# A hybrid RG-LRU, HGRN2 and mixture-of-experts layer on one core: the vector engine's head loop written out, and four pieces of work put elsewhere

## The chip, the core and the metric

The kernel runs on one core of one Trainium2 chip. The metric is the device time of one execution in microseconds (us). The core has a matrix engine (TensorE: PE for its matrix products, PEld for its weight loads), VectorE (DVE), ScalarE (ACT), GpSimd (POOL) and SyncE (SP), which here issues nearly all transfers from the chip's memory. Every engine runs its own program in order, and the programs meet in semaphores: one engine waits until another has counted a semaphore up far enough.

## The reference

One backbone layer on 256 latent tokens and 256 context tokens, width 1024, all in float32. Cut to what matters:

```python
hx = modulate(rmsnorm(x), ...);  hc = modulate(rmsnorm(ctx), ...)      # shift and scale from c @ w_mod
ax, ayx, qx, ffx, fbx, vx, ogx, gax, gbx = split(hx @ w_in)            # the same w_in for hc
ya = RG-LRU of the convolved a, forward and backward                   # 8 heads of 128 channels
yb = HGRN2 of q, f, v, forward and backward, in chunks of 32 tokens    # 8 heads of 128 x 128
pa = (ya * gelu(ay)) @ w_proj_a;  pb = (headnorm(yb) * silu(og)) @ w_proj_b
x  = x + gate1 * ((sigmoid(ga) * pa + sigmoid(gb) * pb) @ w_out)
h2 = modulate(rmsnorm(x), ...)
x  = x + gate2 * moe(h2)      # 4 groups of 8 experts, best group, its best two experts per token
out = rmsnorm(x) * final_g
```

The context is used only for the states from which the latent scans start. `w_mod` has 6 x 1024 columns; the first 2048 are needed ahead of the heads, the other 4096 (gates, second shift and scale) are worked out beside the heads, 512 columns in each head.

## The kernel before, in words

The program has four stages. A short one normalises and turns the tokens. Then come the eight **heads**, one after another. Then the two **projections** with `w_proj_a` and `w_proj_b`, tile m of 128 output columns from 0 to 7, the merge and the product with `w_out`. Last is the **expert stage**: every expert's three weight matrices (2 MB each) pass through a ring of ten buffers.

The order of the work is written out by hand on each engine; there is no scheduler. What sets it in a head:

- **PE** makes the products with `w_in` for the head. Line 732 (`down_k`) is a whole product over eight blocks of 128 rows. Line 804 (`product`) is half of one: the forget gates of latent and context tokens are made in seven half products (FG1 to FG7) instead of eight, with sums of weight blocks and sums of token blocks. Lines 818 and 819 are the RG-LRU gate products of direction 0 and 1, which need the convolved `u` (DVE line 1658). Line 876 (`value_product`) does the same trick for the values `v`, two heads at a time: in an **even** head five such half products, in an **odd** head two. After the values come the transposed keys (825), the attention blocks (838 to 856), the row sums of the modulation (755), and the products with the state (864).
- **DVE** copies the head's parameters (1645), convolves (1656, 1658), adds up the forget gates out of the bank sums (1682, the outputs `fg_out` OUT15, OUT16, OUT_FC, OUT_BC, OUT_BX), forms the decays, and at the end of the head scans (1749) and writes the two results `ya_g` and `yb_g` (line 1854). Between the forget-gate sums it works on the modulation: `mod_products(first, end)` multiplies blocks `first` to `end` of the 512 `w_mod` columns by a scalar and adds them to block 0 (line 1670 for block 0, 1672 for the others). They are eight operations in a head in all, each waiting for the one ahead, and the last raises `modr_out`, for which PE's row sums at line 755 wait. `ratios(d)` is three operations: add (1730), reciprocal (1731), multiply (1732). `evacuate(d)` takes the masked attention blocks of direction d out of the bank (1785, 1788, and for d = 1 line 1791). Line 1836 picks the modulation rows out of the bank and raises `mod_out`.
- **POOL** multiplies gate and `u` for each direction (`gates(d)`, line 675), forms products with the decays (`prods`), the sums of forget-gate weights for the next head (`weight_sums`, 652 to 657), and the scan inputs (`inputs`, 691). `value_sums` (662, 664, 666, 667) forms the four sums of value weights for a pair of heads; PE's second value product needs the first two of them, its fifth all four.
- **SP** issues each transfer when its buffer is free.

DVE's heads are a loop with two heads in its body (odd and even are different code), so four passes; POOL's are a loop of three passes of two, and the last two heads are written out.

```python
with dve.Fori(0, HEADS - 1, 2) as h:
    for odd in range(2):
        head(h + odd, h, odd)
```

Of the kernel before, what the change touches and what calls it, by code (L numbers as in the profile page):

```python
# [22 lines left out]
P = 128  # L23
KT = D // P
# [62 lines left out]
def build(nc, x, c, ctx_in, c_ctx, w_mod, b_mod, norm1_g, w_in, conv_w, conv_b, lru_wa, lru_ba, lru_wx, lru_bx,  # L87
# [9 lines left out]
    with ExitStack() as es:  # L97
# [19 lines left out]
        def S(name):  # L117

            if name not in sems:
                sems[name] = es.enter_context(nc.semaphore(name))  # L120
            return sems[name]
# [225 lines left out]
        def this(h, d=None):  # L347
            return h + 2 if d is None else 2 * h + d + 3

        def last(h, d=None):  # L350
            return h + 1 if d is None else 2 * h + d + 1
# [42 lines left out]
        def _(sp):  # L394
# [134 lines left out]
            def proj_loads(m):  # L529

                if m >= 4:
                    sp.wait_ge(S(f"proj_mm{m % 2}"), m // 2 - 1)
                sp.dma_start(wp[m % 4][0], wpa_v[:, :, P * m:P * m + P]).then_inc(S(f"wp_in{m % 4}"), 16)
                sp.dma_start(wp[m % 4][1], wpb_v[:, :, P * m:P * m + P]).then_inc(S(f"wp_in{m % 4}"), 16)
# [13 lines left out]
            proj_loads(3)  # L548
            sp.wait_ge(S("yb_out"), this(HEADS - 1))
            sp.wait_ge(S("ya_out"), this(HEADS - 1))  # L550
            for i in range(2):
                sp.dma_start(wo[i], wo_v[:, :, F * i:F * i + F]).then_inc(S("wo_in"), 16)
            proj_loads(4)
            proj_loads(5)
            proj_loads(6)
            proj_loads(7)
            fetch(2)
# [52 lines left out]
        def _(pool):  # L610
# [48 lines left out]
            def value_sums(pair):  # L659

                pool.wait_ge(S("in_v"), (pair + 2) * 16)
                pool.tensor_tensor(vs1, v21, v22, ALU.add).then_inc(S("v_w"), 1)
                pool.wait_ge(S("v_w"), v_w_at(pair, 1))
                pool.tensor_tensor(vs2, vs1, v11, ALU.subtract).then_inc(S("v_w"), 1)
                pool.wait_ge(S("v_w"), v_w_at(pair, 2))
                pool.tensor_tensor(vs4, v12, vs2, ALU.subtract).then_inc(S("v_w"), 1)
                pool.tensor_tensor(vs3, v11, v21, ALU.subtract).then_inc(S("v_w"), 1)

            def head(h, more):

                def gates(d):

                    pool.wait_ge(S("ig_out"), this(h, d))
                    pool.wait_ge(S("conv_out"), this(h))
                    pool.tensor_tensor(ig[d], ig[d], u, ALU.mult).then_inc(S("iu_out"), 1)  # L675

                def prods(d):
                    pool.wait_ge(S("ec_out"), this(h, d))
                    pool.tensor_tensor(ec[d], ec[d], kk[d][:, T:], ALU.mult)
                    pool.wait_ge(S("exps_out"), this(h, d))  # L680
                    pool.wait_ge(S("qs_out"), this(h))
                    pool.tensor_tensor(e3[d], e3[d], qs, ALU.mult).then_inc(S("qe3_out"), 1)
                    pool.wait_ge(S("fac_out"), this(h, d))
                    pool.wait_ge(S("qe3_out"), this(h, d))
                    pool.tensor_tensor(chunks(q0[d]), chunks(e3[d]), per_chunk(fac[d][:, 2, :]), ALU.mult).then_inc(S("q0_out"), 1)

                def inputs(d):

                    pool.wait_ge(S("sqrt_out"), this(h, d))
                    pool.wait_ge(S("iu_out"), this(h, d))  # L690
                    pool.tensor_tensor(tz[d], tz[d], ig[d], ALU.mult).then_inc(S("b_out"), 1)

                gates(0)
                gates(1)
                prods(0)
                prods(1)
                if more:
                    pool.wait_ge(S("lv_out"), this(h, 1))
                    weight_sums(h + 1)
                inputs(0)  # L700
                inputs(1)
# [5 lines left out]
            pool.wait_ge(S("hx_out"), KT + 3)  # L707
            pool.tensor_tensor(ht4, x_hi, ht2, ALU.subtract).then_inc(S("tok_copy"), 1)
            with pool.Fori(0, HEADS - 3, 2) as h:
                value_sums(h)  # L710
                head(h, True)
                head(h + 1, True)
            value_sums(HEADS - 2)
            head(HEADS - 2, True)
            head(HEADS - 1, False)

            pool.wait_ge(S("rstd_out"), 3)
# [830 lines left out]
        def _(dve):  # L1548
# [87 lines left out]
            def head(h, pair, odd):  # L1636
# [40 lines left out]
                def fg_sum(dst, bank_, other, n_mm, n_out, needs=None):  # L1677

                    dve.wait_ge(S("fg_mm"), fg_at(h, N_FG, n_mm))
                    if needs:  # L1680
                        dve.wait_ge(S("fg_out"), fg_at(h, N_FG_OUT, needs))
                    tt(dst, bank_[:, 0:T], other, ALU.add).then_inc(S("fg_out"), 1)  # L1682
# [2 lines left out]
                dve.wait_ge(S("prod_q"), last(h, 1))  # L1685
                dve.wait_ge(S("qe3_out"), last(h, 1))
                tt(qs, PJ[1][:, 0:T], sq, ALU.mult).then_inc(S("qs_out"), 1)
                fg_sum(fg15, TB, fg1, FG5, OUT15)
                mod_products(0, 2)
                fg_sum(fg16, KB, fg1, FG6, OUT16)  # L1690
                mod_products(2, 5)
                fg_sum(gg[0][:, T:], TB, fg16, FG3, OUT_FC, OUT16)
                mod_products(5, 6)
                fg_sum(gg[1][:, T:], KB, fg15, FG7, OUT_BC, OUT15)

                def forget(d):
# [27 lines left out]
                    tt(d4[d].rearrange("p (c s) -> p c s", s=CH),  # L1724
                       lc[:, :, tot:tot + 1].to_broadcast([P, NCH, CH]), lc, ALU.subtract).then_inc(S("lc_out"), 1)

                def ratios(d):

                    dve.wait_ge(S("tz_out"), this(h, d))
                    link(ts(rc[d], tz[d], 1.0, None, ALU.add))  # L1730
                    link(dve.reciprocal(rc[d], rc[d]))
                    tt(tz[d], tz[d], rc[d], ALU.mult).then_inc(S("w_out"), 1)

                def prods(d):
# [57 lines left out]
                    i.then_inc(S("att_out"), 1)  # L1792

                forget(0)
                mod_products(6, 7)
                fg_sum(gg[1][:, 0:T], KB, fg1, FG4, OUT_BX)
                mod_products(7, KT).then_inc(S("modr_out"), 1)
                forget(1)
                def values(dst, bank_, other, n_mm, needs=None):

                    dve.wait_ge(S("v_mm"), v_at(pair, n_mm))
                    if needs:
                        dve.wait_ge(S("v_out"), v_at(pair, needs))
                    if dst is v_x or dst is v_c:
                        dve.wait_ge(S("inter_mm"), last(h, 1))
                    if other is None:
                        i = cp(dst, bank_[:, 0:T])
                    else:
                        i = tt(dst, bank_[:, 0:T], other, ALU.add)
                    i.then_inc(S("v_out"), 1)  # L1810
# [18 lines left out]
                    values(v_c, TB, v16, V3)  # L1829
                prods(1)  # L1830
                levels(1)
                ratios(0)
                evacuate(0)
                dve.wait_ge(S("mod_mm"), this(h))
                dve.wait_ge(S("mod_out"), last(h))
                stt(mod_acc, OB[:, 0:P], col(V_PICK), mod_acc, ALU.mult, ALU.add).then_inc(S("mod_out"), 1)
                evacuate(1)
                ratios(1)
                scans(0)
# [14 lines left out]
                stt(yb_g[:, h, :], on, col(V_HG), sog, ALU.mult, ALU.mult).then_inc(S("yb_out"), 1)  # L1854
                assert link.n == N_STEP, link.n

            with dve.Fori(0, HEADS - 1, 2) as h:
                for odd in range(2):
                    head(h + odd, h, odd)


            def merge(i, b, first):
# [325 lines left out]
```

## Time and profile before

| | |
|---|---|
| median of 3 runs | 975.27 us (971.31 to 975.5) |
| the profiled execution, its own time | 970.89 us |
| its span in the trace | 968.8 us |
| PE busy | 810.9 us, 84% |
| DVE busy | 416.5 us, 43% |
| ACT busy | 271.2 us, 28% |
| POOL busy | 133.8 us, 14% |
| transfers | 285.68 MB, 295 GB/s over the span |

The span is the time from the first to the last instruction of the profiled execution. "Busy" counts the engine's own work; an engine that waits for a semaphore is idle. The shares are averages over stages with different limits: the heads end at about 434.6 us, the projections and the product with `w_out` at about 522 us, and the rest is the expert stage.

### The profile page before, as it was taken

The page shows a single profiled execution, that of the slowest core. Times are in us where ns is not written, and L with a number is a line of the kernel's source. Part 1 is how long each engine was busy: PE and PEld are TensorE (multiplying, and loading weights), DVE is VectorE, ACT ScalarE, POOL GpSimd, SP SyncE. Part 2 cuts the span into 40 slices and gives each one's busy share as a digit, 9 for nine tenths or more (in the row PEclk, how much of TensorE's full clock was granted, in tenths as well). Part 3 has the DMA queues.
Part 4 walks back from the last instruction along what each step waited for, and adds up shares of the span by engine and source line. Part 5 has one row for each costly group of instructions (what it writes and reads, how often), then busy time and mean ns, then how long its engine had stood idle before and what let it go on. Part 6 is the DMA issues. An engine that isn't in the chain of part 4 may idle for free.

```text
span 968.8 us, 13449 instructions
## 1 busy us (share of the span) xinstructions
PE 810.9 (84%) x4788; PEld 538.5 (56%) x4788; DVE 416.5 (43%) x973; ACT 271.2 (28%) x547; POOL 133.8 (14%) x157
## 2 busy tenths in 40 slices
PE   3989998999899989999999856574865646799796
PEld 1678887888788879888857322122231301333432
DVE  3687797769676968782125610401001000010102
ACT  5344454445343635360005111001010100101202
POOL 1453151306040514120000000000000000000000
PEclk9999999999999999999999997688887877899999
DMA  9945472446344634479986999999999999999996
GB/s 369 320 104 184 110 218 78 150 133 206 86 126 139 199 95 124 135 237 365 360 340 249 377 428 427 429 426 429 426 429 428 427 427 428 428 428 429 426 423 255
DMA packets 128568, 285.68 MB, mean 295 GB/s; under 512 B 6944, under 2 KB 101376, under 8 KB 114816
## 3 DMA queue, kind: packets, MB, share of 16 engines
q1 hardware_dynamic: 127424, 283.56, 77.6%
q10 hardware_dynamic: 1088, 1.43, 0.4%
q8 instruction: 28, 0.46, 0.2%
q14 instruction: 28, 0.23, 0.1%
HBM read 283.91 MB, written 1.06 MB: 294 GB/s over the span
## 4 chain that ended last, share of the span: by engine, by line
PE 48%; DMA 31%; DVE 8%; issue 5%; SPq 3%; ACT 2%; POOL 2%; ACTq 1%; DVEq 0%; POOLq 0%
DMA arena<-in_w 29%; PE bank L732 12%; PE bank L1137 9%; PE bank L804 8%; PE bank L876 4%; PE bank L1046 3%; PE bank L1148 3%; PE bank L1012 2%; DMA arena<-in_w_proj_b 2%; SPq L591 1%; DVE arena L1672 1%; DVE arena L1774 1%; PE bank L764 1%; PE bank L818 1%; PE bank L819 1%
## 5 line engine op out<-in xcount | busy, mean ns | idle before, releaser
L1137 PE MATMUL bank<-arena 128*32 128x512 f32 (+1 forms) x1024 | 146.9, 679 | 80.3 <-DMA arena<-in_w 80.3
L732 PE MATMUL bank<-arena 128*128 128x256 f32 (+1 forms) x896 | 204.7, 379 | 0.1
L732 PEld LDWEIGHTS bank<-arena 128*128 128x128 f32 x896 | 167.8, 190 | 23.9 <-issue 0.4
L1137 PEld LDWEIGHTS bank<-arena 128*32 128x32 f32 (+1 forms) x1024 | 39.4, 127 | 185.5 <-issue 99.6
L2010 DVE TENSOR_TENSOR arena<-arena,bank 128x512 f32<-128x512 f32 x9 | 9.3, 1034 | 237.5 <-PE bank L1137 237.5
L804 PE MATMUL bank<-arena 128*128 128x256 f32 x448 | 102.6, 383 | 4.7 <-DVE arena L1682 4.7
L1148 PE MATMUL bank<-arena 128*32 128x512 f32 (+1 forms) x512 | 74.6, 683 | 31.8 <-DMA arena<-in_w 31.8
L804 PEld LDWEIGHTS bank<-arena 128*128 128x128 f32 x448 | 85.0, 191 | 18.3 <-DVE arena L1682 3.8
L719 POOL TENSOR_TENSOR arena<-arena,rstd 128x512 f32<-128x512 f32 x1 | 1.0, 1041 | 529.0 <-DVE rstd L2152 529.0
L2019 DVE TENSOR_TENSOR arena<-bank,arena 128x512 f32<-128x512 f32 x18 | 12.5, 692 | 127.6 <-PE bank L1148 127.6
L1148 PEld LDWEIGHTS bank<-arena 128*32 128x32 f32 (+1 forms) x512 | 19.5, 127 | 79.9 <-issue 47.0
L1498 ACT ACTIVATE arena<-bank 128x512 f32<-128x512 f32 x9 | 5.4, 597 | 191.7 <-PE bank L1137 191.7
L876 PE MATMUL bank<-arena 128*128 128x128 f32 x448 | 52.0, 275 | 0.0
L876 PEld LDWEIGHTS bank<-arena 128*128 128x128 f32 x448 | 51.6, 192 | 0.4
L1672 DVE SCALAR_TENSOR_TENSOR arena<-arena 128x512 f32<-128x512 f32 x56 | 46.8, 836 | 0.8
L1502 ACT ACTIVATE arena<-bank 128x256 f32<-128x256 f32 x9 | 3.4, 383 | 138.0 <-PE bank L1199 138.0
L1490 ACT ACTIVATE arena<-bank,arena 128x128 f32<-128x128 f32 x72 | 27.0, 456 | 30.5 <-PE bank L1124 30.5
L1124 PE MATMUL bank<-arena 128*128 128x128 f32 x288 | 33.8, 276 | 1.3 <-DVE arena L1990 1.3
L1124 PEld LDWEIGHTS bank<-arena 128*128 128x128 f32 x288 | 32.9, 192 | 3.1 <-DVE arena L1990 2.2
L675 POOL TENSOR_TENSOR arena<-arena 128x258 f32<-128x258 f32 x16 | 16.0, 1004 | 128.5 <-ACT arena L1354 128.5
L1158 PE MATMUL bank<-arena 128*128 128x512 f32 x64 | 29.6, 605 | 0.0
L1012 PE MATMUL bank<-arena 128*128 128x256 f32 x128 | 29.0, 380 | 0.4 <-DMA arena<-in_w_proj_b 0.4
(343 smaller groups left out, 1079.7 us busy)
## 6 DMA issues: line engine op xcount, KB each, us to landing
arena<-in_w SPq DMA_DIRECT2D x89, 2048.0 KB, 29.2
arena<-in_w_in SPq DMA_DIRECT2D x72, 512.0 KB, 5.1
arena<-in_w_mod SPq DMA_DIRECT2D x11, 2048.0 KB, 11.3
arena<-in_w SPq DMA_DIRECT2D x10, 1024.0 KB, 14.4
arena<-in_w_proj_a SPq DMA_DIRECT2D x8, 512.0 KB, 7.1
arena<-in_w_proj_b SPq DMA_DIRECT2D x8, 512.0 KB, 7.2
arena<-in_w_out SPq DMA_DIRECT2D x2, 2048.0 KB, 15.5
arena<-in_x SPq DMA_DIRECT2D x4, 512.0 KB, 9.2
```

The costliest lines, as they stand in the source:

```text
L675: pool.tensor_tensor(ig[d], ig[d], u, ALU.mult).then_inc(S("iu_out"), 1)
L732: i = mm(dst, w(k), rhs(k), start=k == 0, stop=k == KT - 1)
L804: i = mm(dst[:, 0:T], w[:, k, :], rhs[:, k, :], start=fresh and k == 0, stop=k == HALF - 1, skip_group_check=True)
L876: i = mm(dst[:, P * t:P * t + P], tokens[:, k, P * t:P * t + P], w[:, k, :], start=fresh and k == 0 and t == 0, stop=k == HALF - 1, skip_g ...
L1012: mm(PJ[1 - b][:, 0:T], wp[m % 4][0][:, k, :], ya_g[:, k, :], start=k == 0, stop=k == KT - 1)
L1046: i = mm(bank[to][:, 0:wide], merged[:, k, P * t:P * t + P], wo[c0 // F][:, k, c0 % F:c0 % F + wide], start=k == 0, stop=k == KT - 1)
L1124: i = mm((GX if half else UX)[:, P * k:P * k + P], xn[t][:, P * kt:P * kt + P], hot[:, t, :], start=t == 0, stop=t == 1)
L1137: i = mm(acc[w * b:w * b + w, :], xg[:, k, w * b:w * b + w], wtile(kind, b, u)[:, k, :], start=k == 0, stop=k == KT - 1)
L1148: i = mm(acc[w * b:w * b + w, :], gT[:, f, w * b:w * b + w], wtile("w2", b, u)[:, f, 512 * hf:512 * hf + 512], start=f == 0, stop=f == F / ...
L1158: i = mm(ACC[t][hf][:], ct[:, t, :], ys[:, hf, :], start=u == 0, stop=False, skip_group_check=True)
L1490: i = A(xg[:, kt, :], (GX if half else UX)[:, P * k:P * k + P], ACT.Identity, scale=mod_pk[:, 1, kt:kt + 1], bias=mod_pk[:, 0, kt:kt + 1])
L1672: i = stt(acc, wmod[:, k, :], c_k, acc, ALU.mult, ALU.add)
```

## The change

Four edits.

1. **DVE's head loop is written out**: the same function is called eight times with numbers in place of a loop register, so that the branch back and the register arithmetic for waits are gone. In the program DVE has 862 rows instead of 497.
2. **In the first head DVE works in another order.** OUT16 comes right behind OUT15, blocks 0 and 1 of the modulation behind it, then the other forget-gate sums with nothing between them; block 2 follows `forget(1)`, and blocks 3 to 7 stand behind `ratios(0)`, ahead of `evacuate(0)`. In the odd heads (1, 3, 5, 7) `evacuate(0)` and line 1836 stand ahead of the multiply that ends `ratios(0)`.
3. **POOL forms the value sums of a pair inside the even head**, between `gates(0)` and `gates(1)`, instead of ahead of it, which was right behind the odd head's `inputs(1)`.
4. **SP issues the two `w_out` transfers** behind the projection weights of tiles 4 and 5 instead of ahead of them.

```diff
@@ block.sync
             sp.wait_ge(S("yb_out"), this(HEADS - 1))
             sp.wait_ge(S("ya_out"), this(HEADS - 1))
+            proj_loads(4)
+            proj_loads(5)
             for i in range(2):
                 sp.dma_start(wo[i], wo_v[:, :, F * i:F * i + F]).then_inc(S("wo_in"), 16)
-            proj_loads(4)
-            proj_loads(5)
             proj_loads(6)
             proj_loads(7)
@@ block.gpsimd
-            def head(h, more):
+            def head(h, more, pair=None):
...
                 gates(0)
+                if pair is not None:
+                    value_sums(pair)
                 gates(1)
...
             with pool.Fori(0, HEADS - 3, 2) as h:
-                value_sums(h)
-                head(h, True)
+                head(h, True, h)
                 head(h + 1, True)
-            value_sums(HEADS - 2)
-            head(HEADS - 2, True)
+            head(HEADS - 2, True, HEADS - 2)
             head(HEADS - 1, False)
@@ block.vector
+                first = h == 0
                 fg_sum(fg15, TB, fg1, FG5, OUT15)
+                if first:
+                    fg_sum(fg16, KB, fg1, FG6, OUT16)
                 mod_products(0, 2)
-                fg_sum(fg16, KB, fg1, FG6, OUT16)
-                mod_products(2, 5)
+                if not first:
+                    fg_sum(fg16, KB, fg1, FG6, OUT16)
+                    mod_products(2, 5)
                 fg_sum(gg[0][:, T:], TB, fg16, FG3, OUT_FC, OUT16)
-                mod_products(5, 6)
+                if not first:
+                    mod_products(5, 6)
                 fg_sum(gg[1][:, T:], KB, fg15, FG7, OUT_BC, OUT15)
...
-                def ratios(d):
+                def ratios(d, between=None):
...
                     link(dve.reciprocal(rc[d], rc[d]))
+                    if between:
+                        between()
                     tt(tz[d], tz[d], rc[d], ALU.mult).then_inc(S("w_out"), 1)
...
                 forget(0)
-                mod_products(6, 7)
+                if not first:
+                    mod_products(6, 7)
                 fg_sum(gg[1][:, 0:T], KB, fg1, FG4, OUT_BX)
-                mod_products(7, KT).then_inc(S("modr_out"), 1)
+                if not first:
+                    mod_products(7, KT).then_inc(S("modr_out"), 1)
                 forget(1)
+                if first:
+                    mod_products(2, 3)
...
-                ratios(0)
-                evacuate(0)
-                dve.wait_ge(S("mod_mm"), this(h))
-                dve.wait_ge(S("mod_out"), last(h))
-                stt(mod_acc, OB[:, 0:P], col(V_PICK), mod_acc, ALU.mult, ALU.add).then_inc(S("mod_out"), 1)
+                def first_out():
+                    evacuate(0)
+                    dve.wait_ge(S("mod_mm"), this(h))
+                    dve.wait_ge(S("mod_out"), last(h))
+                    stt(mod_acc, OB[:, 0:P], col(V_PICK), mod_acc, ALU.mult, ALU.add).then_inc(S("mod_out"), 1)
+
+                if odd:
+                    ratios(0, first_out)
+                else:
+                    ratios(0)
+                    if first:
+                        mod_products(3, KT).then_inc(S("modr_out"), 1)
+                    first_out()
...
-            with dve.Fori(0, HEADS - 1, 2) as h:
-                for odd in range(2):
-                    head(h + odd, h, odd)
+            for h in range(HEADS):
+                head(h, h - h % 2, h % 2)
```

How the instructions stand now. First DVE in head 0, from the product `qs` (line 1687) on; 1682 is a forget-gate sum, 1670 and 1672 are modulation blocks, `ISA` and `REGISTER_ALU` serve the waits of the loop. Before:

```order
L1687 TENSOR_TENSOR arena<-bank,arena 128x256
L1679 ISA
L1682 TENSOR_TENSOR arena<-bank,arena 128x256
L1665 REGISTER_ALU
L1670 TENSOR_SCALAR arena<-arena 128x512
L1560 REGISTER_ALU
L1672 SCALAR_TENSOR_TENSOR arena<-arena 128x512
L1560 REGISTER_ALU
L1679 REGISTER_ALU
L1682 TENSOR_TENSOR arena<-bank,arena 128x256
L1672 SCALAR_TENSOR_TENSOR arena<-arena 128x512
```

After (1706 and 1707 are `forget`, lines 1701 and 1702 before):

```order
L1687 TENSOR_TENSOR arena<-bank,arena 128x256
L1682 TENSOR_TENSOR arena<-bank,arena 128x256 x2
L1670 TENSOR_SCALAR arena<-arena 128x512
L1672 SCALAR_TENSOR_TENSOR arena<-arena 128x512
L1682 TENSOR_TENSOR arena<-bank,arena 128x256 x2
L1706 TENSOR_SCALAR arena<-arena,hp 128x512
L1707 TENSOR_SCALAR arena<-arena 128x512
L1682 TENSOR_TENSOR arena<-bank,arena 128x256
L1706 TENSOR_SCALAR arena<-arena,hp 128x512
L1707 TENSOR_SCALAR arena<-arena 128x512
L1672 SCALAR_TENSOR_TENSOR arena<-arena 128x512
```

Six modulation blocks have left the place between the forget-gate sums: one stands at the end here, five further down. Second, DVE in an odd head, where `ratios(0)` and `evacuate(0)` meet; 1785, 1788 and 1836 became 1792, 1795 and 1848, and 1730 to 1732 became 1735, 1736 and 1739. Before:

```order
L1730 TENSOR_SCALAR arena<-arena 128x258
L1560 REGISTER_ALU
L1731 RECIPROCAL arena<-arena 128x258
L1560 REGISTER_ALU
L1732 TENSOR_TENSOR arena<-arena 128x258
L1785 COPY_PREDICATED arena<-head_tab,bank 128x256
L1788 COPY arena<-bank 128x2x128
L1836 SCALAR_TENSOR_TENSOR arena<-bank,hp,arena 128x128
```

After:

```order
L1735 TENSOR_SCALAR arena<-arena 128x258
L1736 RECIPROCAL arena<-arena 128x258
L1792 COPY_PREDICATED arena<-head_tab,bank 128x256
L1795 COPY arena<-bank 128x2x128
L1848 SCALAR_TENSOR_TENSOR arena<-bank,hp,arena 128x128
L1739 TENSOR_TENSOR arena<-arena 128x258
```

The multiply moved behind line 1848. Third, POOL at the start of an even head (here the last one), as a difference; 675 is `gates`, 662 to 667 are the value sums:

```order
+L675 TENSOR_TENSOR arena<-arena 128x258
 L662 TENSOR_TENSOR arena<-arena 128x512
 L664 TENSOR_TENSOR arena<-arena 128x512
 L666 TENSOR_TENSOR arena<-arena 128x512
 L667 TENSOR_TENSOR arena<-arena 128x512
-L675 TENSOR_TENSOR arena<-arena 128x258 x2
+L675 TENSOR_TENSOR arena<-arena 128x258
 L679 TENSOR_TENSOR arena<-arena 128x256
```

The four value sums stood ahead of both gate products and now stand between them.

## Rows read from the trace of the kernel before

**Rows 1.** Windows: PE, PEld, DVE, ACT, POOL busy, clock, DMA share, GB/s.

```profile
152.43:251.66 99.23, 96.34 (x564) 84.39 (x565) 77.13 (x168) 46.79 (x92) 30.38 (x32) 1.00 0.49 144
...
570.00:968.00 398.00, 280.02 (x1718) 103.96 (x1710) 38.85 (x99) 42.09 (x101) 1.04 (x1) 0.86 0.99 418
```

**Rows 2.** Waits of PE over the whole span: total, times, longest.

```profile
PE bank L1137 <- DMA arena<-in_w: 80.3, 12, 11.1
...
PE bank L818 <- DVE arena L1658: 7.5, 3, 2.6
...
PE bank L804 <- DVE arena L1682: 4.7, 2, 3.4
...
PE bank L864 <- DVE arena L1836: 1.0, 3, 0.3
...
PE bank L1012 <- DMA arena<-in_w_proj_b: 0.4, 1, 0.4
```

**Rows 3.** Waits of DVE for issue, over the whole span.

```profile
DVE hp L1645 <- issue: 9.7, 3, 4.0
...
DVE arena L1656 <- issue: 7.0, 3, 2.5
```

**Rows 4.** Timeline of DVE, end of head 3 and start of head 4.

```profile
235.10 0.74 DVE L1749 TENSOR_TENSOR_SCAN arena<-arena 128x256 f32<-128x256 f32 x1
...
236.48 1.74 DVE L1749 TENSOR_TENSOR_SCAN arena<-arena 128x256 f32<-128x256 f32 x1 [0.64 <-POOL arena L691]
...
243.00 0.49 DVE L1854 SCALAR_TENSOR_TENSOR arena<-arena,hp 128x256 f32 x1 [0.16 <-DVE arena L1851]
...
246.41 0.18 DVE L1645 COPY hp<-par 128x23 f32 x1 [2.92 <-issue]
...
249.04 0.61 DVE L1656 TENSOR_SCALAR arena<-arena,hp 128x256 f32<-128x256 f32 x2 [2.45 <-issue]
```

**Rows 5.** Timeline of POOL, head 3's gates(1) and the first value sum for head 4.

```profile
210.79 1.26 POOL L675 TENSOR_TENSOR arena<-arena 128x258 f32<-128x258 f32 x1 [5.10 <-ACT arena L1354]
...
236.40 1.27 POOL L662 TENSOR_TENSOR arena<-arena 128x512 f32<-128x512 f32 x1
```

**Rows 6.** Timeline of PE, head 4's first gate product.

```profile
251.66 0.70 PE L818 MATMUL bank<-arena 128*128 128x258 f32 x2 [2.56 <-DVE arena L1658]
```

**Rows 7.** Timeline of DVE, modulation products early in head 0.

```profile
49.12 2.54 DVE L1672 SCALAR_TENSOR_TENSOR arena<-arena 128x512 f32<-128x512 f32 x1
...
52.13 4.21 DVE L1672 SCALAR_TENSOR_TENSOR arena<-arena 128x512 f32<-128x512 f32 x3
```

**Rows 8.** Timeline of PE, its two waits in head 0.

```profile
52.31 1.97 PE L804 MATMUL bank<-arena 128*128 128x256 f32 x8 [1.35 <-DVE arena L1682]
...
58.52 3.58 PE L804 MATMUL bank<-arena 128*128 128x256 f32 x8 [3.37 <-DVE arena L1682]
```

**Rows 9.** Timeline of POOL, one value sum in head 0.

```profile
52.87 1.42 POOL L664 TENSOR_TENSOR arena<-arena 128x512 f32<-128x512 f32 x1
```

**Rows 10.** Timeline of DVE, head 0, last operation of ratios(0).

```profile
80.14 0.94 DVE L1732 TENSOR_TENSOR arena<-arena 128x258 f32<-128x258 f32 x1
```

**Rows 11.** Timeline of POOL, last weight sum in head 0.

```profile
82.17 1.27 POOL L657 TENSOR_TENSOR arena<-arena 128x512 f32<-128x512 f32 x1
```

**Rows 12.** Timeline of PE, head 0, the modulation row sums.

```profile
83.80 0.42 PE L755 MATMUL bank<-arena,ones 128*32 128x128 f32 x8
```

**Rows 13.** Timeline of DVE, head 3, a modulation product and the last forget-gate sum.

```profile
210.71 0.74 DVE L1672 SCALAR_TENSOR_TENSOR arena<-arena 128x512 f32<-128x512 f32 x1
...
211.97 0.42 DVE L1682 TENSOR_TENSOR arena<-bank,arena 128x256 f32<-128x256 f32 x1 [0.51 <-PE bank L804]
```

**Rows 14.** Timeline of PE, head 2, its five value products.

```profile
164.64 9.09 PE L876 MATMUL bank<-arena 128*128 128x128 f32 x80
```

**Rows 15.** Timeline of DVE, head 2, the first value sum out.

```profile
169.34 0.42 DVE L1809 TENSOR_TENSOR arena<-bank,arena 128x256 f32<-128x256 f32 x1
```

**Rows 16.** Timeline of SP, issue of the fifth w_proj_a tile.

```profile
445.23 2.99 SPq L533 DMA_DIRECT2D arena<-in_w_proj_a  x1
```

## The prediction

> **What bounds the kernel now.** I read the busy times by stretch first. In one pair of heads PE works 96.3 of 99.2 us at full granted clock, DVE 77; in the expert stage the DMA engines are busy 0.99 of the time and PE 280 of 398 us [rows 1]. So the heads are PE's and the experts are the memory's. The list of PE's waits says what PE still loses: 7.5 us in three waits at line 818 for the convolution, 4.7 us in two at line 804 for forget-gate sums, 1.0 us in three at line 864 for line 1836, 0.4 us at line 1012 for projection weights; the 80.3 us at line 1137 are the expert weights [rows 2]. Only those first four, 13.6 us in all, can be won by moving other engines' work. Then I read what makes DVE late at the three waits. In the whole span it has 9.7 us and 7.0 us of idle time "for issue" at lines 1645 and 1656, three times each [rows 3]: nothing was awaited, instructions did not come. The timeline shows the place: `yb_g` of head 3 is done at 243.5, the parameter copy starts at 246.41 after 2.92 us of nothing, the convolution at 249.04 after another 2.45 [rows 4]. That is the loop's branch back; inside a pass, between heads of the same pair, no such row exists. PE gets to its gate product at 251.66 - 2.56 = 249.10 and waits for the convolution [rows 6].
>
> **Edit 1, the loop written out.** It removes three branches back, with 16.7 us of DVE time [rows 3]. PE gets from them what it waits, 7.5 us [rows 2], no more. Check of what is late next: from the start of the convolution to PE's product are 251.66 - 249.04 = 2.6 us [rows 4, 6]; started at about 243.8, it is done by 246.4, 2.7 us ahead of PE. So the whole 7.5 goes, and even a fetch pause of 2.5 us left at this place would cost nothing. Term: **-7.5**; bounds -7.5 and 0.
>
> **Edit 3, the value sums.** What leaves the odd head's end: beside the first sum (236.40 to 237.67) DVE's scan took 1.74 us instead of 0.74 [rows 4, 5]. It ended at 238.22, 0.55 behind the sum's end: it stood until POOL's operation was over, and then ran. This helps only the path that edit 1 has already freed; it adds at least 1.0 us to the 2.7 of slack and nothing to the sum. What arrives: POOL's gap ahead of `gates(1)` is 5.10 us in head 3 [rows 5], and four sums take 4 x 1.27 = 5.1 alone, 4 x 1.42 = 5.7 beside DVE's modulation products [rows 5, 9]. They start where the gap starts, 210.79 - 5.10 = 205.7, and end near 211.4. DVE has two forget operations and a modulation product (0.74 at 210.71) to do ahead of the sum OUT_BX at 211.97, with 0.51 us of idle between [rows 13]. If line 1702 stands until 211.4, then takes 0.3, and the product stands behind `gates(1)` (0.6) and takes 0.55, OUT_BX starts near 212.9, 0.9 late. The chain from there (sigmoid, logarithm, scans, value sum) has little slack: PE's fourth value product of five starts at about 164.64 + 3/5 x 9.09 = 170.1, and DVE's sum for it ends at 169.76 [rows 14, 15], 0.3 us. So 0.6 us a head. This holds for heads 2, 4 and 6: **+1.8**. Bounds: 0, if DVE gets in between two sums; above, if each side stands for the whole of the other's operation, the five operations of DVE and the six of POOL in this stretch come one after another and OUT_BX is 1.9 late, 1.6 x 3 = 4.8. I take the lower middle, because beside DVE POOL's sums grew only from 1.27 to 1.42 [rows 9].
>
> The Trainium skill (SBUF — State Buffer, "Who interferes with whom") speaks against this edit: a VectorE instruction with two SBUF inputs and a GpSimd instruction that reads SBUF lock each other out for a whole instruction, whoever starts first. The scan agrees for DVE's side; POOL's 1.42 is less than the page would give. By the page alone the sum below would be -6.1 instead of -9.1.
>
> **Edit 2, the first head.** PE's two waits of 1.35 and 3.37 us are here [rows 8]. They come from modulation products beside POOL: 2.54 us for one, 4.21 for three, instead of 0.74 [rows 7, 13], in front of the sums that PE needs. Put ahead of them, OUT16 can be made as soon as PE's product for it is done, and OUT_BC needs only PE's next one; both waits go: **-4.7**. The price stands later. Five modulation products now stand behind `ratios(0)`, and PE's row sums at 83.80 wait for the last. In the time of the old trace: `ratios(0)` ends at 81.08 [rows 10]; the first product stands behind POOL's third weight sum (until 82.2), ends at 82.75; the second behind the fourth, 82.17 + 1.27 = 83.44 [rows 11], ends at 84.0; three more of 0.77 end at 86.3. PE waits 86.3 - 83.8 = 2.5 [rows 12], where before DVE was idle. Term **+2.5**; bounds 0.7 (five times 0.77 from 80.6, POOL in no one's way) and 4.3 (five times 1.40 from 81.1). The value sums beside `forget` in this head: 0.2 more. In the odd heads line 1836 goes ahead of a multiply that takes 0.94 beside POOL [rows 10], so `mod_out` comes about 1 us earlier and the waits of 0.33 end: **-1.0**. The multiply ends about 1 us later, but its reader on ACT is behind two table loads and POOL's `inputs` behind the weight sums.
>
> **Edit 4, w_out.** Tile 4's weights, issued at 445.23 [rows 16], stood behind 4 MB in the queue; ahead of them they come in time: **-0.4**. The `w_out` weights come later by about the 10 us that 4 MB take at 418 GB/s [rows 1], but still ahead of tiles 6 and 7 in the same queue, which PE needs first. So nobody can wait for them. The expert loads behind have the same bytes ahead of them as before.
>
> **Does the end move?** The expert stage is bound by its transfers, whose start is set by buffers that PE and DVE free. When those events come earlier, the whole stream does. Head time therefore passes to the end one for one.
>
> **Sum.** -7.5 - 4.7 - 1.0 - 0.4 + 1.8 + 2.5 + 0.2 = **-9.1 us**. The profiled execution's own time is 970.89, two us above its span and 4.4 below the median of the runs, 975.27; two of the three runs lie near 975. Nothing in one profile explains that difference, so I take the saving from the median: **966 us** (from the profiled execution it is 961.8). With the bounds of edits 2 and 3 the saving is 4.3 to 12.7.
>
> **Rivals.**
> - *The value sums stall the even heads* by the whole-operation lock: saving 6.1 or less, 969. For it: the scan's 1.74 us; against: 1.42 for POOL. 0.15, a fifth of it under 0.5%.
> - *The larger saving*: DVE slips between POOL's operations and the five products cost 0.7: 12 us, 963. Against it: 4.21 us for three products. 0.10.
> - *The saving stays in the heads.* If a transfer that doesn't hang on PE bounded the expert stage, the time would be 975 as before. For it: 0.99 DMA share. Against: the ring's loads wait for PE there. 0.09.
> - *Slower: instructions come late in the straight code.* 862 rows instead of 497, none of them repeated, have to be fetched beside the weights. One late fetch of 2.5 us [rows 4] in each head, in the stretch with 0.3 us of slack, costs 8 x 2.2 = 17.6: 975.3 + 8.5 = 984. It decides from 1.1 us in each head. Against it: all of DVE's large pauses for issue are at the branch [rows 3], and the first pass through the loop's body, which was new code too, has none. 0.06.
> - The forecast itself, a saving of 6.5 to 11.5: 0.60.
>
> No change can be told from 0.5% (4.9 us) here. Faster by more: 0.60 + 0.10 + 0.12 = 0.82. Within: 0.03 + 0.09 = 0.12. Slower: 0.06. The range goes from 958.5, the largest saving from the lower level of the runs, to 971.5, the smallest from the median.
>
> **What would show it.** DVE's list of waits without "issue" at 1645 and 1656; PE without the wait at 818, with none at 804 in head 0 and a new one of about 2.5 us at 755 in head 0; value sums of 1.3 to 1.7 us inside even heads, and PE waits of 0.6 us at line 876 in heads 2, 4 and 6; pairs of heads of about 96.9 us instead of 99.2. The prediction is wrong if new pauses for issue stand in the middle of heads, if PE waits over 1.5 us at 876, or if the expert stage starts 9 us earlier and ends at the same time.

## The result

| | median, us | lowest to highest |
|---|---|---|
| before, 5 runs | 971.48 | 969.19 to 975.5 |
| changed, 5 runs | 964.19 | 962.79 to 964.32 |

The ratio is 0.9911, 95% interval 0.9882 to 0.9941: 0.9% faster, 7.3 us between the medians. The profiled execution of the changed kernel took 964.32 us, 6.6 less than that of before (970.89). Of its page, the span, the engines' busy time and one of the two queues that bring instructions, whose packets fell from 28 to 18:

```profile
span 962.3 us, 13146 instructions
...
PE 814.2 (85%) x4788; PEld 540.1 (56%) x4788; DVE 418.4 (43%) x973; ACT 271.7 (28%) x547; POOL 134.7 (14%) x157
...
q14 instruction: 18, 0.15, 0.0%
```

The same row of the page of before:

```profile
q14 instruction: 28, 0.23, 0.1%
```

PE is busy 3.3 us longer than before (810.9); what went is idle time. PE's waits, against [rows 2]:

```profile
PE bank L1137 <- DMA arena<-in_w: 80.5, 12, 12.2
...
PE bank L755 <- DVE arena L1672: 3.1, 1, 3.1
...
PE bank L876 <- DVE arena L1821: 1.5, 3, 0.5
...
PE bank L986 <- ACT arena L1411: 0.7, 3, 0.2
...
PE bank L804 <- POOL arena L710: 0.3, 1, 0.3
```

The 7.5 us at line 818, the 1.0 us at 864 and the 0.4 at 1012 are gone, and of the 4.7 at 804 only 0.3 is left. New are 3.1 us at 755 (head 0), 1.5 us at 876 in three waits (heads 2, 4, 6) and 0.7 us at 986, where ACT is a little late in three odd heads. The waits for expert weights are what they were. The end of head 3 on DVE, against [rows 4]:

```profile
234.76 0.75 DVE L1756 TENSOR_TENSOR_SCAN arena<-arena 128x256 f32<-128x256 f32 x1 [0.64 <-POOL arena L691]
...
238.83 0.48 DVE L1874 SCALAR_TENSOR_TENSOR arena<-arena,hp 128x256 f32<-128x256 f32 x1
...
239.42 0.18 DVE L1645 COPY hp<-par 128x23 f32<-128x23 f32 x1
...
239.64 0.61 DVE L1656 TENSOR_SCALAR arena<-arena,hp 128x256 f32<-128x256 f32 x2
```

The copy at line 1645 starts 0.1 us after `yb_g`, where 2.92 us passed before, and the convolution at once behind it; DVE has no row "for issue" at 1645 or 1656 left. The second scan, which took 1.74 us beside the first value sum, takes 0.75.

The heads of the two traces are best compared from one root-mean-square product (PE line 986) to the next; the start of head 0 is its first gate product (818).

| from the trace, us | head 0 | odd heads 1, 3, 5 | even heads 2, 4, 6 | head 7 | its end to w_out | to the first expert product | to the end |
|---|---|---|---|---|---|---|---|
| before | 44.98 | 45.82 to 45.84 | 53.32 to 53.41 | 45.22 | 56.60 | 39.90 | 438.2 |
| changed | 44.61 | 45.62 to 45.64 | 51.46 to 51.60 | 45.22 | 55.91 | 39.72 | 438.4 |

Even heads give 1.8 us each, odd heads 0.2 each, the projections 0.7. Head 0, whose order was changed most, gives 0.4. The expert stage starts 6.7 us earlier, is as long as before, and ends 6.5 earlier.

### The profile page after: what moved, and what is told of

Its sections match the earlier page's. It is cut to its first block, busy times and chain, and to the rows that moved or that the text cites. A ratio compares the mean times of both kernels' runs of the same rounds, so it can differ in the third digit from the quotient of the medians.

```text
span 962.3 us, 13146 instructions
## 1 busy us (share of the span) xinstructions
PE 814.2 (85%) x4788; PEld 540.1 (56%) x4788; DVE 418.4 (43%) x973; ACT 271.7 (28%) x547; POOL 134.7 (14%) x157
## 4 chain that ended last, share of the span: by engine, by line
PE 56%; DMA 29%; DVE 7%; SPq 2%; ACT 2%; issue 2%; ACTq 1%; POOL 0%; POOLq 0%; DVEq 0%
DMA arena<-in_w 29%; PE bank L732 17%; PE bank L804 9%; PE bank L1137 9%; PE bank L1148 3%; PE bank L1046 3%; PE bank L1012 3%; PE bank L876 3%; SPq L591 2%; DVE arena L1672 1%; PE bank L838 1%; PE bank L764 1%; DVE arena L1736 1%; DVE arena L1739 1%; PE bank L856 1%
## 5 line engine op out<-in xcount | busy, mean ns | idle before, releaser
L1672 DVE SCALAR_TENSOR_TENSOR arena<-arena 128x512 f32<-128x512 f32 x56 | 49.9, 891 | 0.9
## 6 DMA issues: line engine op xcount, KB each, us to landing
arena<-in_w SPq DMA_DIRECT2D x10, 1024.0 KB, 14.7
```

Of the source, the lines that this page charges most:

```text
L1672: i = stt(acc, wmod[:, k, :], c_k, acc, ALU.mult, ALU.add)
```

## The experiments

Ten runs: nine further kernels, and the changed one again. Ratios are to the kernel before, measured beside each, with 95% intervals; three of the ten ran only once and have none. Where two kernels differ by 1 or 2 us, the times alone seldom tell, and the traces have to.

**1. Edit 1 alone** (the kernel before with the loop written out).

```diff
-            with dve.Fori(0, HEADS - 1, 2) as h:
-                for odd in range(2):
-                    head(h + odd, h, odd)
+            for h in range(HEADS):
+                head(h, h - h % 2, h % 2)
```

> The kernel before with edit 1 alone: DVE's eight heads written out, everything else as it was. If the branch back makes DVE late, PE's three waits at line 818 (7.5 us) go and nothing else does: ratio 0.992, PE still waits 4.7 us at line 804 in head 0 and 1.0 us at line 864. Rival, that the value sums at the end of the odd heads are as much the cause as the branch: waits of some tenths are left at 818, saving under 6 us. Rival, that straight code is fetched late: pauses for issue of over 1 us stand at other places of DVE's list, and the time is that of before or more.

963.19 us, ratio 0.9924 (0.991 to 0.9938). PE's waits, the whole list apart from the prologue, the stages behind the projections and 0.3 us at 1012:

```profile
PE bank L804 <- DVE arena L1682: 4.6, 2, 3.3
...
PE bank L864 <- DVE arena L1836: 1.2, 3, 0.4
```

Line 818 is not among them, and DVE has no pause for issue above 0.6 us. Even heads take 50.59 us instead of 53.35, odd heads 45.89. Edit 1 alone gives the whole gain of the change. The other three edits together, for which the sum had -1.6 us, give nothing on top: the changed kernel is at 964.19, ratio 0.9911. Runs 4, 5 and 8 show what each of them does.

**2. Edit 3 alone** (DVE's loop stays, the value sums move).

```diff
                 gates(0)
+                if pair is not None:
+                    value_sums(pair)
                 gates(1)
```

> The kernel before with edit 3 alone: DVE's loop and its branch stay, POOL's value sums stand between the two gates. The value sums held DVE up by about 2.2 us at the end of an odd head (three operations), PE's waits there are 2.5 us each. If both causes are worth nearly the same and cover one another, the three waits shrink to about 0.3 us each, 6.5 us are won there and about 1.5 us are lost again at line 876: ratio about 0.995. Rival, that only the branch counts: PE's waits at 818 stay near 2.5 us and the kernel gets slower by 1 to 2 us.

977.28 us, ratio 1.0066 (1.0052 to 1.0079): 6.2 us slower, where the less favourable theory said 1 to 2. Both fell. DVE's pauses for issue, against [rows 3], and the end of head 3, against [rows 4]:

```profile
DVE hp L1645 <- issue: 12.5, 3, 4.5
...
DVE arena L1656 <- issue: 9.7, 3, 3.4
```

```profile
243.43 0.48 DVE L1854 SCALAR_TENSOR_TENSOR arena<-arena,hp 128x256 f32 x1 [0.16 <-DVE arena L1851]
...
247.91 0.18 DVE L1645 COPY hp<-par 128x23 f32 x1 [4.00 <-issue]
...
251.53 0.61 DVE L1656 TENSOR_SCALAR arena<-arena,hp 128x256 f32<-128x256 f32 x2 [3.44 <-issue]
```

DVE is 2.2 us earlier against PE (`yb_g` ends 4.9 us behind line 986, 7.15 before), as expected. But it then stands 4.00 + 3.44 us instead of 2.92 + 2.45, and the convolution starts 12.56 us behind line 986, where it was 12.70. What was won ahead of the branch was lost in it, and PE still waits 7.1 us at line 818 (7.5 before). A pause of fixed length was assumed, in the prediction too, and it is not one.

The 6.2 us come from elsewhere. Against before, head 0 takes 0.6 us more, since its longer wait at 804 grew from 3.37 to 3.98 us, and heads 2, 4 and 6 take 1.4, 2.1 and 1.7 us more. In head 2 PE has a new wait at 804, for a sum that DVE makes late beside POOL's value sums. In heads 4 and 6 the granted clock fell to half behind the wait at 818, which it had not done in the trace of before. PE in heads 2 and 4, and the window behind the second wait (the clock is the number ahead of the last two, DMA share and GB/s):

```profile
161.86 1.99 PE L804 MATMUL bank<-arena 128*128 128x256 f32 x8 [1.28 <-DVE arena L1682]
...
254.16 1.17 PE L818 MATMUL bank<-arena 128*128 128x258 f32 x2 [2.43 <-DVE arena L1658]
```

```profile
254.30:257.60 3.30, 3.30 (x8) 2.66 (x9) 3.11 (x7) 1.35 (x3) 0.74 (x1) 0.50 0.00 0
```

So what fixes when the instructions are there? In the trace of before the transfers of 238 to 252 (40 slices of 0.35 us) are:

```profile
GB/s 386 410 380 380 392 374 383 334 339 297 291 288 291 291 291 291 284 146 7 0 44 117 306 345 344 313 53 0 0 0 0 0 0 23 0 0 0 0 0 0
...
q14 instruction: 3, 0.02, 0.6%
```

Weights pass at 284 to 410 GB/s until 244, and again at up to 345 GB/s from 245.7 to 247; DVE stands from 243.5 to 249.0. The page counts three packets of instructions on the same 16 DMA engines in this stretch. That they stand behind the weights is so far only a guess; run 3 tests it.

**3. A quieter branch** (run 2, and in odd heads the 2 MB of `w_mod` issued only when DVE has made the next head's copy).

```diff
+                late = ahead == 1
+                if not late:
                     done("mod_mm", h, ahead)
                     load_mod(h, ahead + 1)
                 done("gb_mm", h, ahead)
                 load("ay", h, ahead + 1)
+                if late:
+                    done("hp_out", h, ahead + 1)
+                    load_mod(h, ahead + 1)
```

> The kernel before with edit 3, as in the run with the sums moved alone, and one thing more: in the odd heads SP issues the next head's 2 MB of w_mod only when DVE has copied the next head's parameters, so that fewer weight transfers run while DVE branches back. In the run with the sums moved DVE reached the branch 2.2 us sooner and stood 7.4 us there in head 3 instead of 5.4; its instructions come over the same DMA engines as the weights. If they stand behind the weights, the pause falls to about 5 us or less a branch (22.2 us in three branches with the sums moved, then under 15), and PE's waits at line 818 from 2.4 to under 1 us each. If a pause is a constant of the branch or hangs on something else, it stays at about 7 us. w_mod then comes later, and DVE may wait for it in the even heads; the time of the whole is no matter here.

979.54 us in its one run, on another chip, where before took 972.37. DVE's waits (the lines are five further on in this kernel):

```profile
DVE arena L1675 <- DMA arena<-in_w_mod: 11.0, 3, 3.8
...
DVE hp L1650 <- issue: 8.6, 3, 2.9
...
DVE arena L1661 <- issue: 6.1, 3, 2.1
```

The pauses fell from 22.2 to 14.7 us and PE's waits at the convolution are gone. DVE comes to the branch at the same point as in run 2, 4.95 us behind PE's root-mean-square product, so the traffic is what differs. The first part of the pause at the end of head 3, in run 2 and here (last two numbers: DMA share and GB/s):

```profile
243.90:247.90 4.00, 4.00 (x21) 3.48 (x20) 0.02 (x1) 0.39 (x1) 0.00 (x0) 1.00 0.84 206
```

```profile
245.70:248.30 2.60, 2.60 (x14) 2.27 (x13) 0.00 (x0) 0.00 (x0) 0.00 (x0) 1.00 0.01 3
```

So the branch back costs DVE a fetch that stands behind the weight transfers on their way; 4.9 us a branch remain with `w_mod` out of the way. The 11.0 us for `w_mod` are the price of this kernel's late transfer: PE waits 16.6 us for forget-gate sums, and the kernel is no faster than that of run 2.

**4. Edit 3 undone in the changed kernel.**

> The changed kernel with edit 3 undone: the value sums stand ahead of the even heads again. If edit 3 buys nothing beside edit 1, the DVE delay of 2.2 us at the end of an odd head is covered (PE does not wait at 818) and the 1.5 us of waits at line 876 go: 1.0 to 1.5 us less than the changed kernel, ratio about 0.990. Rival, that the slack at the convolution is gone without it: waits at 818 of up to 1 us each, and no gain.

961.51 us, ratio 0.9901 (0.9887 to 0.9916), 2.7 less than the changed kernel, against a forecast of 1.0 to 1.5. PE has no wait at the convolution and none at the value products; even heads take 50.70 to 50.84 us instead of 51.46 to 51.60, 2.3 us in three heads, and the spans of the two traces, which have the same half clock in head 0, differ by 2.3 us too. With the branch gone the 2.2 us that the value sums cost DVE at the end of the odd head are covered. So edit 3 is a loss. The ratio to the changed kernel's 0.9911 would not show it, as the intervals overlap; the traces do. How it comes, in head 4 of the changed kernel, POOL, DVE and PE:

```profile
249.69 1.72 POOL L662 TENSOR_TENSOR arena<-arena 128x512 f32<-128x512 f32 x1
...
251.49 1.10 POOL L664 TENSOR_TENSOR arena<-arena 128x512 f32<-128x512 f32 x1
...
252.66 1.42 POOL L666 TENSOR_TENSOR arena<-arena 128x512 f32<-128x512 f32 x1
...
254.04 1.27 POOL L667 TENSOR_TENSOR arena<-arena 128x512 f32<-128x512 f32 x1
...
255.27 0.91 POOL L675 TENSOR_TENSOR arena<-arena 128x258 f32<-128x258 f32 x1
```

```profile
254.40 1.20 DVE L1707 TENSOR_SCALAR arena<-arena 128x512 f32<-128x512 f32 x1
...
255.52 1.22 DVE L1672 SCALAR_TENSOR_TENSOR arena<-arena 128x512 f32<-128x512 f32 x1
...
256.77 0.42 DVE L1682 TENSOR_TENSOR arena<-bank,arena 128x256 f32<-128x256 f32 x1
```

```profile
265.21 3.84 PE L876 MATMUL bank<-arena 128*128 128x128 f32 x32 [0.51 <-DVE arena L1821]
```

Line 1707 takes 1.20 us instead of 0.43 and 1672 takes 1.22 instead of 0.74: they end 0.3 and 0.6 us behind a POOL operation. The sum OUT_BX starts at 256.77, 9.68 us behind the head's gate product; in head 3 of before it was 8.85. PE then waits 0.51 us for the value sum, and the five value products take 0.25 us more than in one piece.

**5. Modulation products early in head 0** (the changed kernel; they stand ahead of `prods(1)`).

```diff
+                if first:
+                    mod_products(3, KT).then_inc(S("modr_out"), 1)
                 prods(1)
                 levels(1)
...
                     ratios(0)
-                    if first:
-                        mod_products(3, KT).then_inc(S("modr_out"), 1)
                     first_out()
```

> The changed kernel with one thing else in head 0: modulation products 3 to 7 stand ahead of the second direction's prods. They run while POOL is nearly idle, 0.77 us each, and end before PE's row sums. Theory: the 3.1 us wait at 755 and the half clock behind it go, 5 to 6 us less than the changed kernel, ratio about 0.985. Rival, that the clock did not fall because of the wait: 3 us less only, and attention blocks still at half clock.

958.18 us, ratio 0.9864 (0.9847 to 0.988), 6.0 less than the changed kernel. DVE's five products and PE's row sums:

```profile
69.91 3.88 DVE L1672 SCALAR_TENSOR_TENSOR arena<-arena 128x512 f32<-128x512 f32 x5
```

```profile
78.32 0.42 PE L755 MATMUL bank<-arena,ones 128*32 128x128 f32 x8
```

0.78 us a product and no wait; head 0 takes 38.78 us instead of 44.61. The granted clock is full throughout this head, so of the 5.8 us 3.1 are the wait and 2.6 the half clock behind it; against run 9, where the clock did not fall, it is 3.2.

**6. The same products right ahead of `ratios(0)`.**

> The changed kernel with modulation products 3 to 7 of head 0 ahead of ratios(0) instead of behind it. They then run beside POOL's four weight sums. If POOL's operations hold each product up, five of them take 6 to 7 us from about 72.5 and PE waits about 1 us at line 755, too short for the clock to fall: 4 to 5 us less than the changed kernel. If they did not, they would take 3.9 us and PE would not wait at all. Rival, that the clock falls with any wait here: half clock behind 755 as in the changed kernel, 2 us less only.

961.67 us, ratio 0.9899 (0.9883 to 0.9916), 2.5 less than the changed kernel, head 0 42.05 us.

```profile
72.45 7.44 DVE L1672 SCALAR_TENSOR_TENSOR arena<-arena 128x512 f32<-128x512 f32 x5
```

```profile
79.94 0.43 PE L755 MATMUL bank<-arena,ones 128*32 128x128 f32 x8 [1.81 <-DVE arena L1672]
```

Beside POOL's four weight sums a product takes 1.49 us, twice as long as alone, and the sums take 1.60 to 1.71 us instead of the 1.27 to 1.34 of run 5. The granted clock was half behind PE's wait of 1.81 us: the next four products at line 838 took 1.08 us instead of 0.71. "Too short" was wrong, and the rival of 2 us came nearer than the 4 to 5 us forecast.

**7. The first head's order as before** (`first = False`).

> The changed kernel with the first head's order as before (the other parts stay). By the ledger of the two traces the new order wins PE's waits of 1.35 and 3.37 us and 1.7 us of half clock behind the longer one, and pays 3.1 us of wait and 2.6 us of half clock at line 755: nothing is left, and the time is that of the changed kernel within 1 us, with both waits at 804 back and the first product behind the longer one at half clock. By my prediction the order was worth 2 us, and this kernel would be 2 us slower.

963.73 us, ratio 0.9927 (0.991 to 0.9943): that of the changed kernel, not 2 us more. Both waits are back:

```profile
52.65 1.97 PE L804 MATMUL bank<-arena 128*128 128x256 f32 x8 [1.14 <-DVE arena L1682]
...
58.39 1.99 PE L804 MATMUL bank<-arena 128*128 128x256 f32 x8 [2.90 <-DVE arena L1682]
```

The product behind the longer one took 1.99 us, full clock, where the trace of before shows 3.58 behind its 3.37 us [rows 8]. So that part of the expectation failed. Head 0 takes 42.73 us in this trace, 1.9 less than in the changed kernel's, and its execution is the fastest of the four (962.18).

**8. Edit 4 undone.**

> The changed kernel with edit 4 undone: the w_out loads ahead of tiles 4 and 5. PE's wait for tile 4's weights, 0.4 us before, comes back, perhaps longer, since the heads now end earlier against a queue that moves at its own rate: 0.4 to 1.0 us in the projections (55.5 us from tile 0 to the product with w_out, 56.2 before), nothing in the expert stage. Rival, that the later w_out loads delay the expert loads: the expert stage is shorter here than in the changed kernel.

964.05 us in its one run; PE's wait for tile 4's weights:

```profile
PE bank L1012 <- DMA arena<-in_w_proj_b: 0.8, 1, 0.8
```

From the end of head 7 to `w_out` it is 56.93 us instead of 55.91, and from there to the expert stage 39.7 in both. So edit 4 is worth 1.0 us in the changed kernel, by the trace; the time does not show it, because head 0 took 42.77 us here instead of 44.61. The stage behind `w_out` has the same length in both, so the later `w_out` loads hold nobody up.

**9. The changed kernel again.**

> The changed kernel once more, to see how far the clock behind PE's 3.1 us wait in head 0 repeats. If it falls whenever PE has waited so, attention blocks of direction 1 are at half clock here too, and head 0 takes 42.8 to 44.6 us from its first gate product to its root-mean-square product; at full clock it would be about 42.

961.42 us in its one run. PE in head 0, in the changed kernel's first trace and in this one:

```profile
81.32 0.65 PE L755 MATMUL bank<-arena,ones 128*32 128x128 f32 x8 [3.14 <-DVE arena L1672]
...
81.90 1.22 PE L838 MATMUL bank<-arena 128*128 128x128 f32 x4
```

```profile
81.02 0.43 PE L755 MATMUL bank<-arena,ones 128*32 128x128 f32 x8 [3.13 <-DVE arena L1672]
...
81.38 0.71 PE L838 MATMUL bank<-arena 128*128 128x128 f32 x4
```

The same wait, 3.14 and 3.13 us; behind it four attention products take 1.22 us in the one and 0.71 in the other. Head 0 takes 44.61 and 41.98 us. Two more kernels have this wait, and head 0 takes 44.71 us in the trace of run 4 and 42.77 in that of run 8. So one and the same program differs by up to 2.6 us here, as much as edit 3 costs.

DVE's list shows 1.8 us "for issue" in head 0 in this trace, at line 1792, and 3.3 us in that of run 8, which might be taken for late instructions in the straight code. They are not: in both DVE goes on 0.1 us behind the end of PE's products at line 856, which it reads there, and the list of the changed kernel's first trace names PE for the same gap (3.39 us).

**10. Edit 3 undone and the products early** (runs 4 and 5 together).

> The changed kernel with edit 3 undone and, in head 0, modulation products 3 to 7 ahead of the second direction's prods instead of behind ratios(0). Theory: PE's wait of 3.1 us at line 755 in head 0 goes, and with it the half clock of the 4 to 5 us behind it (2.6 us), so that 5 to 6 us are won beside the 1.0 to 1.5 of the value sums: ratio about 0.984, 6.5 to 7 us under the changed kernel. Rival, that the products only move the wait: the levels of direction 1 come 4 us later, and PE waits for them in its second attention block, gain under 2 us.

955.76 us (955.52 to 956.0), ratio 0.9844 (0.983 to 0.9858), 8.4 less than the changed kernel. It is the best version found: the two savings of 2.7 and 6.0 us nearly add up. Beside run 5 it also prices edit 3 with the clock out of play, as the granted clock never falls in the heads of either trace: the spans are 953.9 and 956.4 us, 2.5 apart.

## Why the prediction was right, and where not

Forecast: 966 us, a saving of 9.1; measured 964.19, a saving of 7.3 between the medians and 6.6 between the profiles. The range and the sign held. That 966 came within 2 us is in part luck: the base, 975.3, was 3.8 too high (over all five runs the median of before is 971.48, close to the profiled execution), and the saving was 1.8 too large; the two errors pull in opposite ways.

- **Edit 1, -7.5: right**, and shown alone (run 1, 7.9 us between medians; no pause was left, so whether one of 2.5 us would have cost nothing stays untested). The reading that DVE's pauses are the branch back holds. The check beside it, that a pause is 2.5 us whenever DVE comes, was wrong (runs 2, 3), which would have mattered had the loop stayed.
- **Edit 3, +1.8: right in mechanism, a little small.** OUT_BX was forecast 0.9 late and came 0.8 late; PE's waits are 1.5 us in all, and even heads lose 0.76 us each, 2.3 (run 4; 2.5 by runs 5 and 10). That each side stands for the whole of the other's operation, the rival of 4.8, is not what happens: beside DVE POOL's four sums took 1.72, 1.10, 1.42 and 1.27 us.
- **Edit 2 in head 0, -4.7 + 2.5 + 0.2: the term that was mis-sized.** PE's waits went as said (4.4 us). The wait at 755 was 3.1 instead of 2.5, because the five products took 1.16 us each, where 1.04 was worked out:

```profile
75.48 5.79 DVE L1672 SCALAR_TENSOR_TENSOR arena<-arena 128x512 f32<-128x512 f32 x5
```

  The sum also left out the clock. PE's granted clock in the changed kernel early in head 0 and right behind the wait (the number ahead of the last two):

```profile
54.40:56.00 1.60, 1.60 (x9) 1.41 (x9) 1.57 (x2) 1.13 (x3) 1.52 (x2) 1.00 1.13 321
...
81.30:83.00 1.70, 1.68 (x12) 1.13 (x12) 0.98 (x3) 0.71 (x2) 0.73 (x1) 0.50 1.17 311
```

  Half clock behind the wait cost up to 2.6 us (run 9 against the first trace). But the trace of before had half clock too, behind its wait of 3.37 us, and that went with the wait: 1.8 us, by the 3.58 us of [rows 8] against 1.89 at full clock, and 0.1 behind it. So between the two traces head 0 won 4.4 and 1.8 us and paid 3.1, 2.6 and 0.2 in the value products: 0.3 in all, measured 0.4, where the forecast was 2.0. Compared at full clock, head 0 takes 42.73 us with the old order (run 7) and 41.98 with the new (run 9): 0.75 us. There the value sums are in both kernels, so the forecast is 4.7 - 2.5 = 2.2; the waits of the old order were 4.0 us and not 4.7, 0.3 of them stayed, and the new one was 3.1 and not 2.5.
- **Odd heads, -1.0: mis-sized.** The waits at 864 went, but 0.7 us at 986 came. The multiply that was put behind line 1836 takes 1.50 us beside POOL (1.09 in its old place), and DVE's second half, `evacuate(1)` and `ratios(1)`, stands behind it. ACT's square, for which PE's root-mean-square product waits, comes later by that. At the end of head 1, before and changed:

```profile
136.40 0.36 ACT L1411 ACTIVATE arena<-bank 128x256 f32<-128x256 f32 x1
```

```profile
136.73 0.36 ACT L1411 ACTIVATE arena<-bank 128x256 f32<-128x256 f32 x1
```

  Counted from the start of the head this is 0.2 us later, while PE gets to the product 0.4 us sooner. The prediction looked at the readers of the multiply and not at DVE's own work behind it. 0.6 is left.
- **Edit 4, -0.4: right, a little small**: 0.7 between the two traces, 1.0 in run 8.
- **The end moves one for one: right.** In every version the stage from `w_out` to the first expert product takes 39.7 to 39.9 us, and from there to the end it is 438.1 to 438.4.

The sum with the measured terms, from the two tables: even heads 5.4, odd heads 0.6, head 0 0.4, projections and the stretch behind 0.9, less 0.5 for a later start of head 0 and 0.2 in the experts: 6.6, and the spans differ by 6.5.

## What to carry to other kernels

When a row says that an engine waited "for issue" at a loop's end, count what the engine behind it waits, not the pause, and write the loop out before moving other work: here that alone was the whole gain. Moving work away from the branch without it won next to nothing there, since the pause grew by nearly what had been saved, and made the kernel slower by what the moved work cost in its new place. A run of VectorE products is cheap where GpSimd is idle, and may take twice as long beside it: choose the place by what GpSimd does at that time, and not only by where VectorE has a gap. When a step is to fill an idle stretch, compute when its last reader comes; five products put in front of PE's row sums took back nearly all that the two removed waits had given. And before a difference of 1 or 2 us is put down to an edit, see whether the granted clock in the two traces is the same.

## What the runs showed of the hardware

- Instruction packets are counted on the DMA engines that carry the weights, and a branch back waits longer beside them: with 2 MB of `w_mod` in flight it cost DVE 7.4 us (run 2), with it out of the way 4.9 (run 3). The eight heads in straight code had no pause for issue above 0.4 us in the changed kernel's first trace or in that of run 1.
- TensorE's granted clock fell from full to half in or behind waits of 3.98 and 2.43 us (run 2), 3.37 (before), 3.14 (first trace of the changed kernel) and 1.81 (run 6), and stayed at full behind 3.13 us (run 9), 2.90 us (run 7) and the 2.56 us of [rows 6]. The length of a wait alone does not tell; what does stays open.
- A VectorE product of 128x512 took 0.74 to 0.78 us alone and 1.16 to 1.49 beside GpSimd's sums; GpSimd's sums of the same size, 1.27 us alone, took 1.10 to 1.72 beside VectorE's work. So VectorE could take twice its time, and GpSimd was not held for the whole of each of VectorE's operations.
